# A hybrid decoder layer on one core: loads moved across stage borders, window copies, late weights and first scores reordered

## What is computed

```python
h = x @ w_in                      # 1024 -> 4096: qa ka va ga (512 each), qb fb ib gb (512 each)
# A: 8 heads of 64, dilated windows (128,1), (512,4), (2048,16), with T5 bias,
#    merged by their softmax denominators; the samples attend to a cache of 2048 keys
# B: 4 heads of 128: f = lb + (1-lb) sigmoid(fb), k = 1-f, q = silu(qb)/sqrt(128)
#    S_t = diag(f_t) S_{t-1} + k_t i_t^T,   o_t = S_t^T q_t, then RMSNorm per head
mix = concat(A * silu(ga), B * silu(gb))
y = LayerNorm(alpha * x + mix @ w_out)
```

## Time and profile before

| | us |
|---|---|
| median of 3 runs | 1870.49 (1869.71 to 1873.99) |
| the profiled execution | 1869.81 |
| its span, first to last instruction | 1868.1 |
| PE, DVE, ACT busy | 1616.3, 787.4, 470.3 |
| mean granted TensorE clock, of full speed | 0.923 |

### The profile page before, as it was taken

The page is one execution under the profiler, slowest core; times in us unless marked ns, Lnnn a source line. Parts: engine busy times, 40 slices in busy tenths (PEclk is TensorE's granted clock), DMA queues, the critical chain, the costliest instruction groups (busy, mean ns, idle before and its releaser), DMA issues. The chain is left out here.

```text
span 1868.1 us, 26055 instructions
## 1 busy us (share of the span) xinstructions
PE 1616.3 (87%) x9834; PEld 1449.9 (78%) x9834; DVE 787.4 (42%) x2024; ACT 470.3 (25%) x1333; POOL 192.7 (10%) x181
## 2 busy tenths in 40 slices
PE   4999999958994997999949889489999999089897
PEld 4999999954783776778749888489999999077775
DVE  4000000004221123212147887155655565489995
ACT  3111111103000113321120221145655565211110
POOL 0000000001210001000000000462614000101111
PEclk9999999977997998999966988689999999599999
DMA  6777777778748579653240220784916111745551
GB/s 219 235 256 252 248 248 248 236 240 267 239 141 263 193 238 330 226 173 101 73 148 1 91 91 24 173 200 99 207 48 158 36 48 32 266 173 214 186 184 40
DMA packets 175293, 319.69 MB, mean 171 GB/s; under 512 B 14819, under 2 KB 114595, under 8 KB 168867
## 3 DMA queue, kind: packets, MB, share of 16 engines
q1 hardware_dynamic: 159036, 220.04, 36.8%
q10 hardware_dynamic: 9216, 66.85, 11.6%
q0 software_dynamic: 6928, 31.31, 6.5%
HBM read 255.02 MB, written 143.89 MB: 214 GB/s over the span
## 5 line engine op out<-in xcount | busy, mean ns | idle before, releaser
L207 PE MATMUL acc<-xhi,whi 128*128 128x424 f32 (+1 forms) x640 | 229.3, 358 | 24.7 <-DVE xlo L187 24.7
L688 PE MATMUL nacc<-nwhi,nxhi 128*128 128x512 f32 (+1 forms) x544 | 218.6, 402 | 23.9 <-DVE nwlo L461 23.1
L207 PE MATMUL acc<-xlo,whi 128*128 128x424 f32 (+1 forms) x640 | 228.6, 357 | 0.0
L207 PE MATMUL acc<-xhi,wlo 128*128 128x424 f32 (+1 forms) x640 | 228.3, 357 | 0.0
L1270 ACT ACTIVATE a_prob<-a_prob,a_stage 128x256 f32<-128x256 f32 (+1 forms) x384 | 174.2, 454 | 192.0 <-DVE a_stage L1245 191.2
L688 PE MATMUL nacc<-nwlo,nxhi 128*128 128x512 f32 (+1 forms) x544 | 213.8, 393 | 0.0
L688 PE MATMUL nacc<-nwhi,nxlo 128*128 128x512 f32 (+1 forms) x544 | 213.7, 393 | 0.0
L1245 DVE CUSTOM_DVE_ANT_0 a_prob<-a_s_ps,a_bias 128x256 f32<-128x256 f32 (+1 forms) x384 | 125.5, 364 | 187.4 <-PE a_s_ps L1308 186.9
L1332 PE MATMUL a_o_ps<-a_v,a_probT 128*128 128x64 f32 x1200 | 157.1, 269 | 8.2 <-DMA a_v<-projN 7.5
L1308 PE MATMUL a_s_ps<-a_khi,a_q 128*128 128x256 f32 (+1 forms) x384 | 157.9, 418 | 6.9 <-POOL a_klo L1217 6.9
L1332 PEld LDWEIGHTS a_o_ps<-a_v,a_probT 128*128 128x128 f32 x1200 | 150.0, 193 | 9.7 <-issue 9.1
(11 more groups left out here) (178 smaller groups left out, 2476.4 us busy)
## 6 DMA issues: line engine op xcount, KB each, us to landing
projT<-stage SPq DMA_DIRECT2D x16, 1056.0 KB, 14.6
out_kwin_s<-in_cache_kT ACTq DMA_DIRECT2D x8, 2048.0 KB, 16.3
nxraw<-in_xT SPq DMA_DIRECT2D x32, 512.0 KB, 7.4
projN<-nstage SPq DMA_DIRECT2D x32, 512.0 KB, 3.4
d_klow<-in_cache_kT SPq DMA_DIRECT2D x8, 2048.0 KB, 10.1
d_vlow<-in_cache_v SPq DMA_DIRECT2D x8, 2048.0 KB
a_raw<-projT POOLq DMA_DIRECT2D x32, 512.0 KB, 9.8
out_kwin_s<-in_cache_kT ACTq DMA_DIRECT2D x8, 2032.0 KB, 22.8
```

The lines of the kernel that those rows point to most:

```text
L207: mm = pe.matmul(acc[:, j, 0:n], w[:, u, k], x[:, k, c0:c0 + n], start=(k == 0 and a == 0), stop=(k == KD - 1 and a == 2))
L688: mm = pe.matmul(acc[0:m, n % 2], x[:, u, k, 0:m], w[:, k, g * H:(g + 1) * H], start=(k == 0 and b == 0), stop=(k == KD - 1 and b == 2))
```

## The change

- `spare`, the space of stage 1's raw x, is allocated around both projections. Once the five x chunks are split, SP loads into it what stage 2 starts with: x of the sample rows, 8 parts of weight piece 0, x tile 0. Stage 2 no longer loads these.
- ACT issues the window copies of a tile after its first chunk, not after its fifth.
- In stage 2 FIRST is HG + 18 = 20 (so LAST = 55), and piece 3 of the weights is loaded ahead of `store(16)`, not behind it.
- `qg`, the space of the recurrence's q and sg, is allocated around stages 2 and 3; in stage 2 the low keys of the samples lie in it, before them the samples' states and masked keys. At n = 56, when all sample scores are done, SP loads the recurrence's masks, identity, and sg and q of segments 0 and 1 into place. Stage 3 takes lb, oml and noml from stage 2's bounds and no longer computes them.
- `decays` makes the four kd first and signals `kd_done`, which PE now waits for instead of `fk_done`.
- In stage 3 the load of sg for segments 2 and 3 waits for the same as that of q. Both stand behind `store(s - 1)`.

```diff
 # project_transposed, sync
+                sp.wait_ge(x_split, NCH)
+                xraw_n, wraw_n = natural_raw(spare)
+                sp.dma_start(xraw_n[:, 0, :, 0:TS], xT[:, :, T:TT]).then_inc(nx_landed[0], 16)
+                for k in range(KD):
+                    sp.dma_start(wraw_n[:, k], w_n[:, k, 0:512]).then_inc(nw_landed[k], 16)
+                sp.dma_start(xraw_n[:, 1], xT[:, :, 0:P]).then_inc(nx_landed[1], 16)
 # project_transposed, scalar
                         nc.scalar.activation(stage[:, u, c0:c0 + n], acc[:, j, 0:n], func).then_inc(bank_free, 1)
-                    shift_window(act, win, ct, copied)
+                        if j == 0:
+                            shift_window(act, win, ct, copied)
 # project_natural
-    FIRST, EACH = HG + 13, 5
+    FIRST, EACH = HG + 18, 5
+    LAST = FIRST + EACH * (NB - 1)
...
-                load_x(0)
-                for k in range(KD):
-                    load_w(0, k)
-                load_x(1)
...
                         if j + 2 < NTL * NPASS:
                             load_x(j + 2)
+                        if j == NTL - 1:
+                            for k in range(KD):
+                                load_w(3, k)
                         store(j)
...
-                    if n == 2 * NTL - 1:
-                        for k in range(KD):
-                            load_w(3, k)
+                    if n == LAST + 1:
+                        sp.wait_ge(qk_done, NB)
+                        for dst, src in ((first["lmask"], a["lmask"]), (first["dmask"], a["dmask"]), (first["ident"], a["ident"])):
+                            sp.dma_start(dst[:], src).then_inc(first["const"], 16)
+                        for b in range(2):
+                            load_segment(sp, projT, b, first["q"], first["sg"], first["qk_landed"])
...
+def load_segment(sp, projT, s, q, sg, landed):
+    u, t0 = s % 2, s * SEG
+    sp.dma_start(sg[:, u], projT[12:16, :, t0:t0 + SEG].rearrange("h p t -> p h t")).then_inc(landed[u], 16)
+    sp.dma_start(q[:, u], projT[8:12, :, t0:t0 + SEG].rearrange("h p t -> p h t")).then_inc(landed[u], 16)
 # hgrn_prompt, scalar
                     for h in range(HB):
-                        nc.scalar.activation(kd[:, u, h], sg[:, u, h], ACT.Identity, bias=oml[:, h:h + 1], scale=noml[:, h:h + 1])
+                        ins = nc.scalar.activation(kd[:, u, h], sg[:, u, h], ACT.Identity, bias=oml[:, h:h + 1], scale=noml[:, h:h + 1])
+                    ins.then_inc(kd_done, 1)
+                    for h in range(HB):
                         ins = nc.scalar.activation(fd[:, u, h], sg[:, u, h], ACT.Identity, bias=lb[:, h:h + 1], scale=oml[:, h:h + 1])
                     ins.then_inc(fk_done, 1)
...
-                act.wait_ge(lbs, 1)
-                nc.scalar.activation(lbp[:], lbp[:], ACT.Exp).then_inc(lbs, 1)
-                act.wait_ge(bounds, 1)
 # hgrn_prompt, vector: the chain of the bounds is gone
-                dve.wait_ge(const, 16 * 4)
-                tt(lbm[:], lbp[:, 0], lbp[:, 1], ALU.max).then_inc(lb_step, 1)
...
-                nc.vector.tensor_scalar(noml[:], oml[:], -1.0, None, ALU.mult).then_inc(bounds, 1)
                 nc.vector.memset(S[:, 0], 0.0).then_inc(s_done, 1)
                 dve.wait_ge(zeroed, 1)
+                dve.wait_ge(const, 16 * 3)
 # hgrn_prompt, tensor
-                    pe.wait_ge(fk_done, s + 1)
+                    pe.wait_ge(kd_done, s + 1)
```

More of the change, by code:

```diff
@@ L51 @@
 LB = 3 * BAND
+XCOLS = 424
 LD = WIN + 2 * NT
@@ L288, in project_natural @@
             table, exp_sb, vec = sb("table", [BUCKETS + 1, HA]), sb("expand_sb", [BUCKETS + 1, NV]), sb("vec", [HA, NV])
-            lbp, lbs_ = sb("s_lbp", [P, 2, HB]), sb("s_lbs", [P, 4, HB])
+            lbp, lbs_ = sb("s_lbp", [P, 2, HB]), first["bounds"]
             masks = sb("s_masks", [TS, NLV + 1, TS], I32)
@@ L794, in _, with hgrn_prompt @@
                         values(s)
-def hgrn_prompt(nc, projT, projN, lbT, level_masks, diag_mask, ident_d, o_b, state_out):
+def load_segment(sp, projT, s, q, sg, landed):
+    u, t0 = s % 2, s * SEG
+    sp.dma_start(sg[:, u], projT[12:16, :, t0:t0 + SEG].rearrange("h p t -> p h t")).then_inc(landed[u], 16)
+    sp.dma_start(q[:, u], projT[8:12, :, t0:t0 + SEG].rearrange("h p t -> p h t")).then_inc(landed[u], 16)
+def hgrn_prompt(nc, projT, projN, o_b, state_out, first):
     NG2 = HB // 2
@@ L821, in hgrn_prompt @@
         t_ps, o_ps, s_ps = ps("t_ps", [P, 512]), ps("o_ps", [P, 2, 512]), ps("s_ps", [P, 2, 512])
-        qk_landed, v_landed, ost_free = ([sem(f"h_{n}{u}") for u in range(2)] for n in ("qk_landed", "v_landed", "ost_free"))
-        const, state_kept = sem("h_const"), sem("state_kept")
-        lbs, bounds, zeroed, lb_step = sem("h_lbs"), sem("h_bounds"), sem("h_zeroed"), sem("h_lb_step")
+        qk_landed, const = first["qk_landed"], first["const"]
+        v_landed, ost_free = ([sem(f"h_{n}{u}") for u in range(2)] for n in ("v_landed", "ost_free"))
+        state_kept, zeroed, kd_done = sem("state_kept"), sem("h_zeroed"), sem("h_kd_done")
         fk_done, q1_done, a_done, upd_done, mask_done = (sem(f"h_{n}") for n in ("fk_done", "q1_done", "a_done", "upd_done", "mask_done"))
@@ new lines, in build @@
+    o_b = dram("o_b", [TT, WB])
+    attn_s = dram("attn_s", [TS, WA])
+    partials = dram("partials", [NC, T, HA, OW])
+    with ExitStack() as whole:
+        _, _, sem = region(whole, nc)
+        copied = sem("win_copied")
+        w_landed = [sem(f"nw_landed{k}") for k in range(KD)]
+        x_landed = [sem(f"nx_landed{u}") for u in range(2)]
+        first = {"const": sem("h_const"), "qk_landed": [sem(f"h_qk_landed{u}") for u in range(2)]}
+        with ExitStack() as ctx:
+            sb, _, _ = region(ctx, nc)
+            spare = sb("spare", [P, 2 * KD * XCOLS])
+            project_transposed(nc, a["xT"], a["w_t"], projT, win, copied, spare, a["w_n"], w_landed, x_landed)
+            first["bounds"] = sb("bounds", [P, 4, HB])
+            first["lmask"], first["dmask"] = sb("lmask", [P, len(PLEVELS), CH // 2], I32), sb("dmask", [P, CH], I32)
+            first["ident"], first["qg"] = sb("ident3", [P, P]), sb("qg", [P, 4 * HB * SEG])
+            halves = first["qg"][:].rearrange("p (a u h t) -> p a u h t", a=2, u=2, h=HB)
+            first["q"], first["sg"] = halves[:, 0], halves[:, 1]
+            project_natural(nc, a, projT, projN, o["kwin_p"], o["vwin_p"], o["kwin_s"], o["vwin_s"], rep_p, rep_d, o_b, attn_s,
+                            o["hgrn_s"], spare, w_landed, x_landed, first)
+            hgrn_prompt(nc, projT, projN, o_b, o["hgrn_p"], first)
```

70 lines of the change are left out of this document (23 added, 47 removed).

## The result

| | before | after |
|---|---|---|
| median | 1870.97 us (1869.71 to 1873.99, 4 runs) | 1843.66 us (1841.56 to 1846.06, 4 runs) |
| the profiled execution; its span | 1869.81; 1868.1 | 1845.5; 1843.8 |
| mean granted clock | 0.923 | 0.931 |

The account below looks back on a forecast made before the run. The kernel was taken as bound by TensorE, full inside the projections, with gains in its gaps at stage seams. Terms 11 + 9.9 + 0.5 + 5 + 11 + 5.8 = 43.2 us gave a median of 1827, range 1814 to 1842.

Parts of the forecast that it names:

- Copies after the first chunk: Seam between the projections: last copies issued 18 us earlier, the store runs alone; 11 us gained, bounds 9 to 12.
- Bytes: 2.8 + 4.1 + 0.5 = 7.4 MB: First projection: bytes moved until the third weight tile lands, 25 us at 301 GB/s; 7 us of slack, cost 0.
- SP's queue would have half of the rate while ACT's copies last: First projection, DMA engines alternating queues by packet: copies out at 68, third weight tile landing at 69 to 70.
- the rival with 0.07: Third weight tile late in the first stage: price 3 to 10 us, 1830 to 1837; chance 0.07.
- Opening, 9.9 us: Second projection's start to first sample scores (L702): early loads make it 33.3 us against 43.2; bounds 6 to 10.5.
- FIRST, 0.5: Second projection: sample attention starts five groups later, the 26 us gap stays; 0 to 1 us gained, 0.5 taken.
- Weights of piece 3, 5 us: Seam of the two passes: weights land about 5 us earlier, PE's gap 9.8 to some 4.8; bounds 3 to 8.
- Given back: Rival: opening's or part of a seam's gain ends at a later unmoved transfer; gain 31, 1839; chance 0.17.
- Segments, masks and bounds, 11 us: Recurrence's start: early loads hidden in the second stage, levelled scores 10.9 us in, not 22.4; bounds 9.5 to 12.
- kd first, 5.8: Recurrence, segments 2 and 3: PE starts after kd's four operations, 2.9 us gained at each; bounds 4 to 7.
- Clock: as left: Recurrence's first segment: PE's granted clock assumed to stay 0.50 in level steps; rival of better clock 1817, chance 0.1.

## Why the prediction was wrong, step by step

- **Copies after the first chunk, 11 us: right at the seam.** 12.4. The store runs alone and lands in 4.8, and the barrier adds less than the 1 us allowed.
- **The step that failed first: "Bytes: 2.8 + 4.1 + 0.5 = 7.4 MB", so the third weight tile "lands at about 69", cost 0.** It counted one tile's copies (issued at 40.80, not at 44). The edit moves the copies of every tile forward, and those of the second tile too were on their way before the third weight tile landed (56.99). With them it is 11.5 MB; at the same 301 GB/s, counted from 44 as in the forecast, that is 38.2 us and a landing at 82.2, and the cast was at 83.58. The run with the copies back has the 7.4 MB of the forecast, 24.6 us from its first load at 48.54: 73.1, and its cast is at 75.21, with 0.98 us lost.
  The time by which the tile was needed was off too, and by luck of the clock: TensorE was done with the second tile at 75.3, not at 77.94, so 73.3 was the last moment and not 76.
  The forecast's other reckoning, "SP's queue would have half of the rate while ACT's copies last", is the deeper error. The turns here go by the packet and not by the byte: from 62 to 72 the two queues moved 70 and 69 packets, but 3.52 and 0.10 MB. From 47.4 to 72 ACT's copies had 7.2 MB of 7.9, and all that SP had issued came behind them. That order gives the landing; the sum of all bytes over the rate comes near it because SP's were the last of them. The run with the copies back shows the turns with smaller packets: from 63 to 68, 290 packets with 1.14 MB for ACT and 295 with 0.53 MB for SP. Moving the tile ahead of SP's own loads removed the wait while the copies ran as before. This was the rival with 0.07, at 3 to 10 us, and it came in at 10.3.
- **Opening, 9.9 us: 7.6.** The mechanism is right. The first matmul came 1.8 us later than put down, since the first cast took 2.26 us; with the clears out of the way the first scores are 34.0 in, against 33.3 forecast and 35.6 measured.
- **FIRST, 0.5: nothing measurable.** The step of attention is moved, not removed; x tile 8's landing varies by more than what was to be had. It came between 33.7 and 37.1 us, from the evacuation of group 15 to that of 16, in the variants above that touch nothing near it.
- **Weights of piece 3, 5 us: right in size, and not had.** The gap itself fell from 9.80 to 2.18. The step that failed is that nothing was asked of the next transfer: an x tile, beside GpSimd's 4 MB, on which VectorE and by way of the probabilities ACT and TensorE hang. The earlier trace rows end at 724.85, and the argument ended there with them. Before, that x tile (issued at 734.89, cast at 744.03) cost TensorE 0.6 us; now it costs 9.4. "Given back" named the mechanism, but for other tiles.
- **Segments, masks and bounds, 11 us: 12.4**, and the loads at n = 56 cost nothing that shows. No table load, and the start is 0.9 us better than worked out.
- **kd first, 5.8: 5.6** from the levelled scores to the attention; undoing it costs 5.6 there.
- **Clock: as left.** 0.50 in the first segment's level steps, 0.931 for 0.923 over the span, which is fewer gaps and no faster step.

The sum: of 43.2 forecast, 24.3 show in the spans. The first projection takes 10.3 of the difference, the second projection behind its opening 8.8 (5.5 not had, 3.3 lost), its opening 2.3, kd first 0.2, and the other stretches return 2.7. Of the 3.3 us lost behind the opening, 0.5 is the seam of passes and 2.8 are the moved attention step (7.0 against 4.2); undoing that step didn't make the kernel faster, so what it costs in all stays within the spread of the runs.

## What to carry to other kernels

When a load is put early, list everything that stands behind it on the same queue, and count all bytes that are on the way until the first of those is needed, including the transfers that another edit of the same change moves there. Ask too for the packets of each queue: here a load with small packets hardly moved beside a copy with large ones. In front of early loads for a later stage goes whatever this stage needs next; here the place of one 0.5 MB transfer was worth 10.9 us of the first projection. When a gap is closed, follow the engine to its next wait before the gain is booked: the second gap grew by what the first had lost, until the bulk copy that nobody waits for was moved out of the crowded stretch.

## What the runs showed of the hardware

- VectorE's first cast (128x512) took 2.26 us, from 414.08, while GpSimd cleared a tile (1.80 us, from 414.25), and 0.43 us with that clear moved away. The Trainium skill (SBUF — State Buffer, SBUF: two separate sides) has the port pair that VectorE and GpSimd share as an exclusive lock, held for the whole instruction; for VectorE it names operations in a mode that uses two ports, or with two inputs in SBUF. These two rows agree with a lock; that the cast ran in such a mode is not shown here.
- A transfer's issue itself takes long when much is on its way. Eight issues of 256 KB took SP 11.39 us beside ACT's copies and 4.20 at the same place in the run with the copies back, where those started only behind them; the issue of the weight tile took 17.12 and 1.86. SP was held for 30 us in the changed kernel.
- Two queues with work at the same time got equal packets and not equal bytes: 70 and 69 packets from 62 to 72 us, ACT's copies 3.52 MB (some 50 KB a packet), SP's queue 0.10 MB (1.5 KB a packet).
- The DMA engines moved 362 to 386 GB/s while 1.02 to 1.03 busy, more than the 301 from which the sum was made. A copy from DRAM to DRAM took part in both.
